# A two-layer decoder trunk on one core: the matmul that adds a sample tile's partial sums stands further on, and the first sample tile has a bank of its own

## The reference

```python
def trunk_layer(x, l, pos, mixer_a, s0, w_in, w_out, ...):
    h = rmsnorm(x, g_mix_pre[l])
    qa, ka, va, qi, ki, wi, qb, kb, vb, gb = project_mixers(h, w_in[l], pos)
    a = mixer_a(qa, ka, va, qi, ki, wi)          # indexer scores, top-k, softmax attention
    b, S = retention_mixer(qb, kb, vb, gb, s0, g_ret[l])
    m = jnp.concatenate([a.reshape(B, T, W_A), b], axis=-1) @ w_out[l]
    x = x + rmsnorm(m, g_mix_post[l])
    f = jnp.square(jax.nn.relu(rmsnorm(x, g_ffn_pre[l]) @ w_up[l])) @ w_down[l]
    x = x + rmsnorm(f, g_ffn_post[l])
    return x, ka, va, ki, S.astype(s0.dtype)
```

## Time and profile before

| | us |
|---|---|
| median of 3 runs | 1653.7 |
| lowest and highest | 1651.63, 1654.96 |
| the profiled execution | 1654.42 |
| its span | 1652.6 |

### The profile page before, as it was taken

One profiled execution on the slowest core, in us unless ns is written; L12 is line 12 of the kernel. 1 busy time (PEld: TensorE's weight loads), 2 busy tenths in 40 slices (PEclk: granted clock), 3 DMA queues, 4 the chain that ended last, 5 costly groups with the idle time before them and its releaser, 6 DMA issues.

```text
span 1652.6 us, 19575 instructions
## 1 busy us (share of the span) xinstructions
PE 1580.8 (96%) x6986; PEld 1101.5 (67%) x6986; DVE 831.6 (50%) x1761; ACT 432.5 (26%) x975; POOL 420.8 (25%) x332
## 2 busy tenths in 40 slices
PE   7999899999999999999989998999999999999995
PEld 4344344478888888888843433445888888888884
DVE  4498556684743002332566984577646420133335
ACT  4312244314422002210142212443244310032100
POOL 0000000113363433353420000010226433343451
PEclk9999999999999999999999999999999999999998
DMA  6135401121422122312123252101233312222211
GB/s 203 63 127 167 146 20 52 53 78 55 153 102 103 72 82 102 103 51 102 63 94 102 77 202 105 52 1 54 81 103 127 105 74 103 102 80 100 77 51 52
DMA packets 52498, 150.26 MB, mean 91 GB/s; under 512 B 8331, under 2 KB 29331, under 8 KB 39091
## 3 DMA queue, kind: packets, MB, share of 16 engines
q1 hardware_dynamic: 44770, 140.65, 24.3%
q10 hardware_dynamic: 7632, 8.36, 1.5%
HBM read 139.79 MB, written 9.02 MB: 90 GB/s over the span
## 4 chain that ended last, share of the span: by engine, by line
PE 76%; DVE 16%; ACT 3%; issue 2%; DMA 2%; SPq 1%; ACTq 0%; DVEq 0%; POOL 0%; POOLq 0%
PE ps L1028 42%; PE ps L690 17%; PE ps L966 7%; DVE arena L1604 1%; DVE x_feat L1753 1%; DVE top L1602 1%; DVE arena L1643 1%; PE ps L694 1%; PE ps L828 1%; ACT arena L1182 1%; DVE s_sb L1751 1%; PE ps L815 1%; PE ps L838 1%; PE ps L649 1%; PE ps L924 1%
## 5 line engine op out<-in xcount | busy, mean ns | idle before, releaser
L690 PE MATMUL ps<-wring,h_feat 128*128 128x512 f32 (+1 forms) x960 | 438.6, 596 | 4.2 <-ACT arena L1182 2.8
L690 PEld LDWEIGHTS ps<-wring,h_feat 128*128 128x128 f32 x960 | 173.3, 193 | 192.7 <-issue 181.2
L1028 PE MATMUL ps<-arena,wring 128*128 128x256 f32 (+1 forms) x1280 | 285.8, 382 | 0.3 <-DVE arena L1832 0.3
L1028 PEld LDWEIGHTS ps<-arena,wring 128*128 128x128 f32 x1280 | 243.1, 190 | 37.7 <-DVE arena L1832 1.1
L1028 PE MATMUL ps<-h_feat,wring 128*128 128x256 f32 (+1 forms) x768 | 176.8, 382 | 2.5 <-DVE arena L1832 2.5
L2086 POOL TENSOR_TENSOR wring<-wring,arena 128x512 f32<-128x512 f32 (+1 forms) x48 | 78.8, 1641 | 341.2 <-PE ps L1028 321.6
L1028 PEld LDWEIGHTS ps<-h_feat,wring 128*128 128x128 f32 x768 | 145.8, 190 | 24.8 <-DVE arena L1832 3.3
L1028 PE MATMUL ps<-mix,wring 128*128 128x256 f32 (+1 forms) x512 | 123.6, 391 | 3.9 <-DVE s_sb L1806 3.9
L1028 PE MATMUL ps<-arena 128*128 128x264 f32 x512 | 119.2, 386 | 0.0
L966 PE MATMUL ps<-mix,wring 128*128 128x256 f32 (+1 forms) x512 | 115.0, 383 | 0.8 <-ACT mix L1242 0.8
L1028 PEld LDWEIGHTS ps<-mix,wring 128*128 128x128 f32 x512 | 99.4, 194 | 20.9 <-DVE s_sb L1806 4.8
(11 more groups left out here) (212 smaller groups left out, 1800.8 us busy)
## 6 DMA issues: line engine op xcount, KB each, us to landing
wring<-in_w_all SPq DMA_DIRECT2D x108, 1024.0 KB, 5.0
arena<-in_cache_k SPq DMA_DIRECT2D x32, 256.0 KB, 5.3
arena<-in_cache_v SPq DMA_DIRECT2D x32, 256.0 KB, 4.3
wring<-in_w_idx SPq DMA_DIRECT2D x4, 648.0 KB, 5.6
x_feat<-in_x SPq DMA_DIRECT2D x4, 520.0 KB, 6.4
o_k_out<-arena ACTq DMA_DIRECT2D x2, 1024.0 KB
o_v_out<-arena ACTq DMA_DIRECT2D x2, 1024.0 KB
arena<-in_state SPq DMA_DIRECT2D x2, 1024.0 KB, 4.9
```

Source lines behind the costliest of these rows:

```text
L690: last = mm(ps[:, proj_bank(n), 0:width], h_feat[:, k, token_cols(t)], wt, start=(k == 0), stop=(k == KD - 1))
L1028: last = mm(out, a[:, j, :], b, start=(opens(n) and j == 0), stop=(j == nk - 1), skip_group_check=True)
```

## The change

`add_parts(n - 1)` stands behind matmul j = 5 of the next tile instead of j = 1; in projection 4 behind j = 2. In layer 0 the first sample tile (n = 4) gets bank 4, so it waits for no read, and the next two tiles, in banks 1 and 0, wait for `proj_read` 2 (before, 4 and 5), since the banks' last users are tiles 1 and 0. All other waits are as before.

```diff
         def proj_bank(n):
-            return n if now[0] == 0 and n < NT else n % 2
+            return n if now[0] == 0 and n < TILES else n % 2
+
+        def bank_taken(n):
+
+            if now[0] == 0 and n < TILES:
+                return None
+            return past(proj_read) + (2 if now[0] == 0 and n in (TILES, TILES + 1) else n - 1)
...
-                    if n == NT and now[0] == 0:
-                        pe.wait_ge(proj_read, 1)
-                    elif n >= 2:
-                        pe.wait_ge(proj_read, past(proj_read) + n - 1)
+                    if n >= 2 and bank_taken(n):
+                        pe.wait_ge(proj_read, bank_taken(n))
...
-                        if j == 1 and n and (i == 0 or tile_order(c)[i - 1] == NT):
+                        if j == (2 if c == 4 else 5) and n and (i == 0 or tile_order(c)[i - 1] == NT):
                             add_parts(n - 1)
```

## The result

| | before | after |
|---|---|---|
| median, us | 1652.66 | 1669.72 |
| lowest and highest | 1651.55, 1654.96 | 1669.18, 1670.89 |
| the profiled execution | 1654.42 | 1669.18 |
| its span | 1652.6 | 1667.4 |
| its mean granted clock | 0.987 | 0.984 |

The changed kernel is slower: ratio 1.0102, 95% interval 1.0085 to 1.012, four runs of each. That is 17 us on the medians and 14.8 us between the two profiled spans.

The account below looks back on a forecast made before the run. The prediction took TensorE, busy 96% of the span, as the bound, so its waits count. Place terms of +5.9 us and lowered clocks of +5.1 gave +11.0 on 1653.7: 1664.7, put down as 1664.5, range 1653 to 1671.

Parts of the forecast that it names:

- L649 at most 1 us: TensorE's waits at the add of partial sums, 9.9 us before, would shrink to at most 1 us.
- (3, 1), a wait of 2.9 for VectorE, once per layer: Projection 3, tile 1: transposes would wait some 2.9 us for VectorE's delayed rope of (2, 4), in both layers.
- (7, 0), 2.8 for ScalarE: Projection 7, tile 0: third group of transposes would wait 2.8 us for ScalarE's copies, once per layer.
- (5, 0), 2.5 at L838: Projection 5, tile 0: the add's wait would become one of about 2.5 us for the softmax step; net +0.6 per layer.
- (6, 0), 1.5 at L828: Projection 6, tile 0: a new 1.5 us wait at attention's scores, yet a net gain of 3.2 us per layer.
- First sample tile near 29, the next at 33: Kernel start: sample tile starts near 29 us, its successor waits for bank 1 until 33; gain 1.5 us.
- (1, 0) of layer 1, +0.8: Projection 1, tile 0, layer 1: transposes wait for the later rope, costing 0.8 us.
- Rival A: Waits at the add simply go, with lowered clocks and 1.5 at the start: 15.6 us faster, 1638; chance of gain 0.08.
- its three conditions: 3.4 us of room at the rope of (2, 4), (7, 0)'s third transposes and (5, 0)'s softmax step; rows showed 0.5, 0.0, 0.1.
- The sum of +5.9: Net of all forecast gains and losses by place over both layers, before lowered clocks behind new waits: +5.9 us.
- three of the six new waits: Of six waits at (3, 1), (5, 0), (7, 0), twice each, three followed by lower clock at 1.7 us each: +5.1.
- Rival E: All six new waits followed by the lowered clock, and more: 1667 to 1671 us, chance 0.17.

Follow-up runs that it names:

- e2: Kernel before with the add moved behind j=5 in projection 2 alone: 1660.23 us beside 1652.87, ratio 1.0043.
- e3: Kernel before with the add moved behind j=5 in projection 7 alone: 1659.04 us beside 1652.87, ratio 1.0038.
- e4: Kernel before with the add moved behind j=5 in projection 5 alone: 1658.74 us beside 1652.87, ratio 1.0033.
- e1: Changed kernel with the add back behind j=1 everywhere, only the first sample tile's new bank left: 1650.57 us beside 1652.87 before, ratio 0.9986.
- e8: e1 with three unused matmuls between the first sample tile and tile (1, 0): 1650.16 us beside 1651.39 for the kernel before, ratio 0.9989.
- e5: Kernel before with the add moved behind j=5 in projection 6 alone: 1649.08 us beside 1651.39, ratio 0.9981.
- e6: Kernel before with the add behind j=3 in projections 5 and 6 alone, no new bank: 1638.70 us beside 1651.44, ratio 0.9918.
- e9: Changed kernel with the add back behind j=1 in projections 2 and 7: 1651.87 us beside 1651.39 for the kernel before, ratio 1.0009.
- e10: Changed kernel with the add behind j=2, 3, 3 in projections 1, 5, 6, else j=1, plus three unused matmuls: 1635.48 us beside 1651.44 before, ratio 0.9895.

## Why the prediction came out as it did

The forecast was 1664.5, the range 1653 to 1671; measured 1669.72. The direction and every new wait were as forecast. The size of the clock's part was not, and the result lies 1.3 us from the upper end of the range.

**The waits, one by one.** *L649 at most 1 us*: 0. *(3, 1), a wait of 2.9 for VectorE, once per layer*: 3.15 and 3.13; the slack of 0.5 us in VectorE's stretch was all there was. *(7, 0), 2.8 for ScalarE*: 2.75. *(5, 0), 2.5 at L838*: 2.34. *(6, 0), 1.5 at L828*: 1.28. *First sample tile near 29, the next at 33*: 29.30 and 33.43. *(1, 0) of layer 1, +0.8*: +0.8. Rival A, by which the waits simply go, falls with each of these; e2, e3 and e4 show its three conditions false one at a time.

**The sum without the clock.** The sum of +5.9 counted 2 x 2.1 us of lowered clock as gained in (6, 0); without that it is +10.1. Measured in S x C: +9.9. By parts, forecast and (measured alone): projection 2 at (3, 1) +5.8 (+4.5 ±0.8), projection 7 +6.0 (+5.5 ±0.4), (5, 0) +1.2 (+2.1 ±0.4; the wait of 0.53 us at L842 ahead of the add, which the forecast had only as a bound, came in full), (6, 0) -2.2 (-2.3 ±0.4), the start -1.5 (-0.4 ±0.4 for the bank alone), (1, 0) +0.8. The five measured parts sum to +9.4. That the sum is so close is in part luck: projection 2 is 1.3 us under its forecast and projection 7 0.5, (5, 0) and the start are 0.9 and 1.1 over.

**The term that was mis-sized is the clock.** Forecast: three of the six new waits followed by the lower level, 1.7 us each, +5.1, and the two stretches in (6, 0) gone, -4.2: net +0.9. Measured net: +5.1 between the profiles, +7 to +8.5 over the runs. Behind the new waits alone it is 13.6 us in the profile; that the net is not further off comes from the three stretches missing elsewhere, which were not forecast. Two things were off. Five of the six waits were followed by it, not three: (3, 1) and (5, 0) in both layers, (7, 0) in layer 0. And three of the five stretches lasted 6.8 us, not the 3.4 that the earlier trace rows had. That such stretches exist stood in the trace before, at 834.4 to 841.2, and I hadn't read it. The 2.1 us that the forecast took for each stretch in (6, 0) were too much as well: it is 3.4 us long with TensorE busy throughout, 1.7. Rival E has the result in its range, 1667 to 1671, though only five of the six waits were followed; the forecast lay 5 us below.
The reading behind "three of six" does not hold either. It took a wait of 2.08 us as safe and one of 2.61 as always followed. Over the six profiles that have each (before, e1, e8, and those of e2 to e5 in which the place is not edited), the first was followed in 3 of 12 places and the second in 9 of 12.
*The start*: forecast -1.5, measured +0.9 in the profile. The earlier sample tile left its own wait of 2.83 us where TensorE had 0.39 before, as the forecast had it, and the lowered stretch lasts 6.8 us where the profile before has 3.4. But e2 to e6 show that 6.8 us is usual there with the old start too. The two profiles with the bank and the add at j = 5 (the change and e9) have (1, 1) at +0.9 and +1.7, the six with the old start at 0 to +2.3, 1.4 on average. So the start gave nothing, in place of 1.5, and did not cost 0.9 either; with the add at j = 1 (e1) some gain is left.

By the Trainium skill, TensorE: Matmul & The Clock Gate, "HAM oscillation", throttled time costs half of its length. The trace agrees where TensorE is busy throughout: in e4 four records take 3.76 us in the stretch and 1.99 outside. At the start, where TensorE is busy for 4.07 of 6.80 us, half of the stretch is too much.

**What stays open.** Why the wait of 2.34 us at L842 was followed by 6.8 us in both layers, in the changed kernel, e4 and e9 alike, and the one of 2.75 us in (7, 0) in layer 0 alone, by 3.4 us in the changed kernel and 6.8 in e3. A difference between them is that behind the first TensorE goes on with sixteen records of 8 columns (L887, 2.42 us); that this matters was not tried. Open too is why the gain at the start in e8 is in the profile and not in the median, why e5 gained nothing from the clock, and where in the kernel the +7 to +8.5 us of the runs lie: by S x (1 - C) the five parts measured alone sum to +4.2 ±2.1.

## What to carry to other kernels

A matmul whose input comes late can go anywhere between the end of that input and the last moment at which its result is not yet wanted: read both off the timeline before moving it. Here two moves to j = 3 lay between them and gained 13 us; the moves to j = 5 lay mostly behind, and the change with them lost 17. Follow the delay on every engine down to the next place where two meet without slack; it was up to six tiles away. And price a new TensorE wait of over 2 us with a chance of the lowered clock behind it, at the longest such stretch in the trace, not the nearest. One profile does not give that chance: what followed the same wait changed from one profile to the next.

## What the runs showed of the hardware

- The stretches at half clock lasted 3.4 or 6.8 us in the twelve profiles, the one at the very end of each apart (14 to 18 us). e8 and e10 have only the shorter length.
- How often a wait of TensorE in the projections was followed by one (begun during the wait or within 2 us of its end), over all profiles that have the wait:

| wait | us | followed | lengths |
|---|---|---|---|
| at the add in (5, 0), j = 1 | 2.08 to 2.10 | 3 of 12 | 3.4 |
| at L838 (L842) in (5, 0), j = 5 | 2.33 to 2.34 | 6 of 6 | 6.8 |
| at the add in (6, 0), j = 1 | 2.61 | 9 of 12 | 3.4 |
| at the transposes in (7, 0), j = 5 | 2.75 | 2 of 4 | 3.4, 6.8 |
| at the transposes of (3, 1), j = 5 | 3.13 to 3.15 | 4 of 4 | 3.4 in layer 0, 6.8 in layer 1 |

- The time that the lower clock takes varies between executions of the same kernel (S x (1 - C) from 15 to 27 us for the kernel before, whose S x C is 1631.5 on average in each session). Comparing S x C separates a change of about a microsecond from that, the standard errors in the table being 0.3 to 0.9.
- Parts whose S x C was measured alone add up: +9.4 of the five, +9.9 for the whole (the moves in (1, 0), (3, 0) and (4, 0) were not measured alone).
